# Chunk decays of a two-direction state-space scan: the two directions' exponents merged by a predicated copy before one exponential, and the diagonal weights made in the in-projection

## The reference

```python
a_cs = jnp.cumsum(a, axis=-1)            # a = dt * A, per chunk of 128 positions
Lmat = segsum_exp(a)                     # exp(a_cs[l] - a_cs[s]) for s <= l, else 0
y_diag = jnp.einsum('bclgn,bcsgn,bgrcls,bcsgrp->bclgrp', Cc, Bc, Lmat, xd)
...
y_f = ssd_scan(xs, dt_f, A[0], Bm, Cm)
y_b = flip(ssd_scan(flip(xs), flip(dt_b), A[1], flip(Bm), flip(Cm)))
y = y_f + y_b + xs * d_skip[:, None]
```

## Time and profile before

| | |
|---|---|
| median of 3 runs | 2932.55 us (2932.18 to 2933.72) |
| profiled execution, span | 2927.1 us |
| PE busy in it | 2844.0 us, 97% |
| DVE busy | 1921.0 us, 66% |
| ACT busy | 1161.9 us, 40% |
| POOL busy | 442.2 us, 15% |
| mean granted TensorE clock | 0.984 of full |
| 16 heads, first exponent product to last evacuation | 454.63 to 531.64 us |

### The profile page before, as it was taken

One profiled execution on the slowest core, in us unless ns is written; L12 is line 12 of the kernel. 1 busy time (PEld: TensorE's weight loads), 2 busy tenths in 40 slices (PEclk: granted clock), 3 DMA queues, 4 the chain that ended last, 5 costly groups with the idle time before them and its releaser, 6 DMA issues.

```text
span 2927.1 us, 34428 instructions
## 1 busy us (share of the span) xinstructions
PE 2844.0 (97%) x13489; PEld 2265.7 (77%) x13489; DVE 1921.0 (66%) x2492; ACT 1161.9 (40%) x1708; POOL 442.2 (15%) x323
## 2 busy tenths in 40 slices
PE   8999999999999999999999999999799999999999
PEld 6767778767778888877767888888676888887887
DVE  6548866656587666765667766776737866666254
ACT  2223325213343333433245565556624433334342
POOL 0420011360004332202000000000000232222020
PEclk7999999999999999999999999999999999999999
DMA  6344475025132222375540111111133222226453
GB/s 216 110 136 151 145 224 194 29 79 201 54 131 80 75 86 87 124 251 183 176 157 18 47 43 43 43 43 45 64 101 101 87 86 87 87 65 203 136 158 116
DMA packets 361686, 326.60 MB, mean 112 GB/s; under 512 B 11501, under 2 KB 319182, under 8 KB 361486
## 3 DMA queue, kind: packets, MB, share of 16 engines
q1 hardware_dynamic: 348486, 271.61, 29.7%
q0 software_dynamic: 12000, 48.61, 4.5%
q10 hardware_dynamic: 1040, 4.19, 0.4%
HBM read 263.88 MB, written 68.35 MB: 114 GB/s over the span
## 4 chain that ended last, share of the span: by engine, by line
PE 90%; DVE 5%; ACT 2%; DMA 1%; issue 1%; POOL 1%; SPq 0%; ACTq 0%; DVEq 0%; POOLq 0%
PE psum_gemm L1953 20%; PE psum_misc L1953 18%; PE psum_gemm L2399 8%; PE psum_gemm L216 6%; PE psum_gemm L217 6%; PE psum_gemm L220 6%; PE psum_misc L2463 3%; PE psum_gemm L2484 3%; PE psum_gemm L2472 3%; PE psum_gemm L318 2%; PE psum_misc L216 2%; PE psum_misc L217 2%; PE psum_misc L220 2%; PE psum_misc L888 1%; PE psum_gemm L2485 1%
## 5 line engine op out<-in xcount | busy, mean ns | idle before, releaser
L216 PE MATMUL psum_gemm<-h_hi,w_hi 128*128 128x512 f32 x816 | 329.3, 404 | 12.0 <-DVE h_lo L401 8.2
L217 PE MATMUL psum_gemm<-h_lo,w_hi 128*128 128x512 f32 x816 | 318.5, 390 | 0.0
L198 ACT ACTIVATE w_hi<-w_raw 128x1024 fp32r<-128x1024 f32 x93 | 97.8, 1055 | 455.1 <-PE psum_gemm L220 321.4
L1878 DVE TENSOR_TENSOR ring_lo<-piece_raw,ring_hi 128x512 fp32r<-128x512 f32 x192 | 137.0, 722 | 206.2 <-ACT ring_hi L1872 205.7
L220 PE MATMUL psum_gemm<-h_hi,w_lo 128*128 128x512 f32 x816 | 251.9, 390 | 0.0
L203 DVE TENSOR_TENSOR w_lo<-w_raw,w_hi 128x1024 fp32r<-128x1024 f32 x93 | 119.1, 1285 | 158.5 <-ACT w_hi L198 158.5
L1872 ACT ACTIVATE ring_hi<-piece_raw 128x512 fp32r<-128x512 f32 x192 | 112.7, 593 | 246.2 <-PE psum_misc L1953 208.3
L1953 PE MATMUL psum_misc<-h_hi,ring_hi 128*128 128x512 f32 x512 | 200.6, 392 | 0.6 <-DVE ring_lo L1878 0.6
L216 PEld LDWEIGHTS psum_gemm<-h_hi,w_hi 128*128 128x128 f32 x816 | 153.2, 188 | 61.5 <-issue 20.8
L1953 PE MATMUL psum_misc<-h_hi,ring_lo 128*128 128x512 f32 x512 | 199.4, 389 | 0.0
L1953 PE MATMUL psum_misc<-h_lo,ring_hi 128*128 128x512 f32 x512 | 199.2, 389 | 0.0
(11 more groups left out here) (422 smaller groups left out, 6792.3 us busy)
## 6 DMA issues: line engine op xcount, KB each, us to landing
ada_w<-in_w_ada SPq DMA_DIRECT2D x28, 1024.0 KB, 5.5
w_raw<-in_f_w_up SPq DMA_DIRECT2D x52, 512.0 KB, 4.9
ffn_act_scratch<-gate_act SPq DMA_DIRECT2D x42, 512.0 KB, 2.6
piece_raw<-in_f_w_down SPq DMA_DIRECT2D x80, 256.0 KB, 3.2
piece_raw<-ffn_act_scratch SPq DMA_DIRECT2D x80, 256.0 KB, 2.9
pair_raw<-in_f_w_up SPq DMA_DIRECT2D x36, 512.0 KB, 5.1
w_raw<-in_e_w_in SPq DMA_DIRECT2D x29, 512.0 KB, 4.5
x_scratch<-x_res SPq DMA_DIRECT2D x3, 4096.0 KB, 12.6
```

The costliest lines, as they stand in the source:

```text
L198: act.activation(w_hi[:, s], w_raw[:, s], ACT.Copy).then_inc(s_hi, 1)
L216: pe.matmul(o, wh, rh[:, k, c], start=(k == 0), stop=False)
L217: pe.matmul(o, wh, rl[:, k, c], start=False, stop=False)
L1878: dve.tensor_tensor(Al[:, idx % 7, 0:n], src, Ah[:, idx % 7, 0:n].bitcast(F32), ALU.subtract).then_inc(s_wl, 1)
```

## The change

For each head only the exponents without a mask are made: 4 products for each direction instead of 6 (`exponent`). The forward plane is `pG[:, 1]` for even heads and `pM[:, 0]` for odd ones, the backward plane is always `pG[:, 0]`. DVE copies the backward plane over the forward one where a 128x128 predicate (`above`, 1 above the diagonal) says so, PSUM to PSUM, for all 8 chunks in one instruction. ACT takes one exponential of the merged plane, and DVE multiplies it by the scores one head later (`weights`). The addition of the two directions is gone. `y_of` has two half planes (`pM[:, 1]`) instead of four; scores and B transposes all use `pM[:, 1]`.

The backward direction's term on the diagonal is now missing from the weights. It is score(l,l) * dt_b, a factor of x, like the skip term; both are put into `yS` ahead: `own_scores` (POOL, two multiplications of 128x1024, elementwise C*B), `own_pe` (PE, 16 products of 128x128 by 1 column which sum them over the state, in the hook of `cumsum_pe`), `own_dve` (DVE, four small instructions, giving `y_w` = dt_b * score + d_skip) and `own_x` (POOL, `yS` = `xS` * `y_w`, one 128x1024 multiplication for each of 8 chunks: chunks 0, 1, 4, 5 behind the store of z tile 6, chunks 2, 3, 6, 7 at the end of `diag_pool`). `evac` adds the head's product to `yS`, and waits for all of these. The six coefficients and the shift splits of `mods_dve` go into `coefs_dve`, at head 8. Of the constants, one select and two copies of POOL are gone.

```diff
                 if j == 5:
+                    own_dve(dve)
                     cumsum_dve(dve)
...
                     ssd_consts(pool)
+                    own_scores(pool)
+                if j == 6:
+                    for c in (0, 1, 4, 5):
+                        own_x(pool, c)
...
-        mask = at("mask", AR + 65, [P, 2, P])
-        maskR = at("mask_r", AR + 66, [P, 2, P], F32R)
-        identR = at("ident_r", AR + 67, [P, P], F32R)
+        above = at("above_diagonal", AR + 66, [P, P])
...
+        y_w = at("own_weight", AR + 75.25, [P, CH, 16])
+        g_own = at("own_score", AR + 75.75, [P, SSM_GROUPS, CH])
+        own = at("own_product", AR + 16, [P, SSM_GROUPS, SEQ])
...
-        E_ = at("decays", 32, [P, 2, 2, SEQ])
+        E_ = at("decays", 32, [P, 2, SEQ])
...
+            pool.affine_select(out=above[:], in_=above[:], compare_op=ALU.is_ge, fill=1.0, base=0,
+                               pattern=[[1, P]], channel_multiplier=-1).then_inc(s_sc, 1)
...
-            pool.tensor_copy(maskR[:], mask[:]).then_inc(s_sc, 1)
-            pool.tensor_copy(identR[:], ident[:]).then_inc(s_sc, 1)
             pool.tensor_copy(selR[:], sel[:]).then_inc(s_sc, 1)
-            pool.wait_ge(s_sc, n + 3)
-            pool.tensor_copy(T2[64:128, :], mask[64:128, 0, P - 1:P].to_broadcast([64, SEQ])).then_inc(s_sc, 1)
-            assert n + 4 == NC_CONST
+            pool.wait_ge(s_sc, n + 1)
+            pool.tensor_copy(T2[64:128, :], above[64:128, P - 1:P].to_broadcast([64, SEQ])).then_inc(s_sc, 1)
...
             pe.wait_ge(s_sc, NC_CONST)
+            own_pe(pe)
             for d in range(2):
                 pe.matmul(pM[:, 0, d * P:(d + 1) * P], tri[:, d], aS[:, :, d * 16:(d + 1) * 16], start=True, stop=True)
             pe.matmul(pM[:, 0, 512:768], ones[:], aS[:], start=True, stop=True).then_inc(s_cs2, 1)
...
         def scores_pe(pe, g):
             for c in range(CH):
                 cc = slice(c * P, (c + 1) * P)
-                last = pe.matmul(pM[:, 1 - g, cc], xbc[:, 8 + g, cc], xbc[:, 10 + g, cc], start=True, stop=True)
+                last = pe.matmul(pM[:, 1, cc], xbc[:, 8 + g, cc], xbc[:, 10 + g, cc], start=True, stop=True)
             last.then_inc(s_bt, 1)
...
         def b_turn(pe, h):
...
-                    last = pe.transpose(pM[:, 1 - h, o:o + P], xbc[:, 8 + g, c * P:(c + 1) * P], ident[:])
+                    last = pe.transpose(pM[:, 1, o:o + P], xbc[:, 8 + g, c * P:(c + 1) * P], ident[:])
...
         def scores_act(act, g):
-            act.wait_ge(s_bt, g + 2)
-            act.activation(Gm[:, g], pM[:, 1 - g], ACT.Copy).then_inc(s_gm, 1)
+            act.wait_ge(s_bt, 2 * g + 2)
+            act.activation(Gm[:, g], pM[:, 1], ACT.Copy).then_inc(s_gm, 1)
...
         def b_copy(dve, h):
-            dve.wait_ge(s_bt, h + 4)
-            dve.tensor_copy(BS[:, 4 * h:4 * h + 4].rearrange("p c n -> p (c n)"), pM[:, 1 - h]).then_inc(s_bc, 1)
-
-        def diff(d):
-            return pG[:, 1 - d]
+            dve.wait_ge(s_bt, 2 * h + 3)
+            dve.tensor_copy(BS[:, 4 * h:4 * h + 4].rearrange("p c n -> p (c n)"), pM[:, 1]).then_inc(s_bc, 1)
+
+        def forward(h):
+            return (pG[:, 1], pM[:, 0])[h % 2]
+
+        backward = pG[:, 0]
+
+        def y_ps(h):
+            return pM[:, 1, (h % 2) * HALF:(h % 2) * HALF + HALF]
 
         def diag_pe(pe):
             def y_of(h):
-                if h >= 4:
-                    pe.wait_ge(s_yev, h - 3)
+                if h >= 2:
+                    pe.wait_ge(s_yev, h - 1)
                 elif h == 0:
-                    pe.wait_ge(s_bc, 2)
-                elif h == 2:
                     pe.wait_ge(s_mods, 4)
                 pe.wait_ge(s_M, h + 1)
-                ps = pM[:, (h % 4) // 2, (h % 2) * HALF:(h % 2) * HALF + HALF]
+                ps = y_ps(h)
                 for c in range(CH):
                     last = pe.matmul(ps[:, c * 64:(c + 1) * 64], W_[:, h % 4, c * P:(c + 1) * P],
                                      xS[:, c, h * 64:(h + 1) * 64], start=True, stop=True)
                 last.then_inc(s_y, 1)
+
+            def exponent(h, d):
+                hd = 16 * d + h
+                dst = backward if d else forward(h)
+                for n in range(2):
+                    pe.matmul(dst[:, n * HALF:(n + 1) * HALF], selR[:, hd:hd + 1].to_broadcast([P, P]),
+                              T2[:, n * HALF:(n + 1) * HALF], start=True, stop=False)
+                for n in range(2):
+                    pick = pickR[:].rearrange("p (c h) -> p c h", h=8)[:, 4 * n:4 * n + 4, h % 8:h % 8 + 1]
+                    last = pe.matmul(dst[:, n * HALF:(n + 1) * HALF], csbT[:, 2 * d + h // 8],
+                                     pick.to_broadcast([P, 4, P]), start=False, stop=True)
+                last.then_inc(s_dif[d], 1)
...
             for h in range(SSM_HEADS):
-                for d in range(2):
-                    hd = 16 * d + h
-                    if h >= 1:
-                        pe.wait_ge(s_exp, 2 * h - 1 + d)
-                    elif d:
-                        ev_in_wait(pe, U_OUTB + 1)
-                    for n in range(2):
-                        pe.matmul(diff(d)[:, n * HALF:(n + 1) * HALF], selR[:, hd:hd + 1].to_broadcast([P, P]),
-                                  T2[:, n * HALF:(n + 1) * HALF], start=True, stop=False)
-                    for n in range(2):
-                        pick = pickR[:].rearrange("p (c h) -> p c h", h=8)[:, 4 * n:4 * n + 4, h % 8:h % 8 + 1]
-                        pe.matmul(diff(d)[:, n * HALF:(n + 1) * HALF], csbT[:, 2 * d + h // 8],
-                                  pick.to_broadcast([P, 4, P]), start=False, stop=False)
-                    for n in range(2):
-                        last = pe.matmul(diff(d)[:, n * HALF:(n + 1) * HALF], identR[:],
-                                         maskR[:, d:d + 1].to_broadcast([P, 4, P]), start=False, stop=True)
-                    last.then_inc(s_dif[d], 1)
-                if h == 0:
+                if h >= 2:
+                    pe.wait_ge(s_exp, h - 1)
+                exponent(h, 0)
+                if h:
+                    pe.wait_ge(s_sum, h)
+                else:
+                    ev_in_wait(pe, U_OUTB + 1)
+                exponent(h, 1)
+                if h in (0, 2):
+                    b_turn(pe, h // 2)
+                elif h == 1:
+                    pe.wait_ge(s_bc, 1)
                     scores_pe(pe, 1)
-                elif h < 3:
-                    b_turn(pe, h - 1)
                 elif h == 3:
-                    pe.wait_ge(s_bc, 1)
+                    pe.wait_ge(s_bc, 2)
                     mods_pe(pe)
-                if h >= 3:
+                elif h == 4:
+                    y_of(0)
+                if h >= 4:
                     y_of(h - 3)
             y_of(SSM_HEADS - 3)
             y_of(SSM_HEADS - 2)
@@ -1475,14 +1490,14 @@
         def diag_act(act):
             act.wait_ge(s_red, ADA_END)
             act.activation(dec[:], totS[:], ACT.Exp).then_inc(s_ex, 1)
+            scores_act(act, 0)
             for h in range(SSM_HEADS):
-                for d in range(2):
-                    if h >= 2:
-                        act.wait_ge((s_sum, s_M)[d], h - 1)
-                    act.wait_ge(s_dif[d], h + 1)
-                    act.activation(E_[:, h % 2, d], diff(d), ACT.Exp).then_inc(s_exp, 1)
-                if h < 2:
-                    scores_act(act, h)
+                if h >= 2:
+                    act.wait_ge(s_M, h - 1)
+                act.wait_ge(s_sum, h + 1)
+                act.activation(E_[:, h % 2], forward(h), ACT.Exp).then_inc(s_exp, 1)
+                if h == 1:
+                    scores_act(act, 1)
 
         def diag_pool(pool):
             pool.wait_ge(s_used, U_OUTB)
@@ -1490,32 +1505,79 @@
             pool.wait_ge(s_fs, 16)
             skew = bass.AP(tensor=f_dram.tensor, offset=P - 1, ap=[[2048, ATT_HEADS], [-1, P], [1, STRIP]])
             pool.dma_start(skew_dram, skew).then_inc(s_fs, 16)
+            pool.wait_ge(s_ex, 3)
+            pool.wait_ge(s_csc, 10)
+            for x in range(2):
+                pool.wait_ge(s_zs[x], 64)
+            for c in (2, 3, 6, 7):
+                own_x(pool, c)
+
+        def own_scores(pool):
+            pool.wait_ge(s_sc, NC_CONST)
+            for x in range(2):
+                pool.wait_ge(s_xsc[x], 4)
+            for g in range(SSM_GROUPS):
+                pool.tensor_tensor(own[:, g], xbc[:, 8 + g], xbc[:, 10 + g], ALU.mult).then_inc(s_own, 1)
+
+        def own_x(pool, c):
+
+            pool.wait_ge(s_ownw, 4)
+            pool.tensor_tensor(as_heads(yS[:, c]), as_heads(xS[:, c]),
+                               y_w[:, c].rearrange("p (h o) -> p h o", o=1).to_broadcast([P, 16, 64]), ALU.mult
+                               ).then_inc(s_own, 1)
+
+        def own_pe(pe):
+            pe.wait_ge(s_own, SSM_GROUPS)
+            for g in range(SSM_GROUPS):
```

(57 more changed lines are left out.)

17 lines of the change are left out of this document (8 added, 9 removed).

## The result

The changed kernel takes 2954.99 us (median of 4 runs, 2944.92 to 2958.6) against 2932.36 before: a ratio of 1.0074, 95% interval [1.0063, 1.0086]. It is slower by about 22 us, where 2932.0 us was forecast and the range ended at 2940.5. The profiled execution has a span of 2956.9 us (2927.1 before) and a mean granted clock of 0.975 (0.984).

A forecast was written before the change was run, and what follows sets the result against it. PE's own work was taken to bound the diagonal stage. A stage gain of 7.2 us against an in-projection loss of 6.7 gave a span of 2926.6 and, with the median 5.4 above it, 2932.0 us; range 2926.0 to 2940.5.

The forecast's parts named there:

- PE's work and the heads: Diagonal stage: dropping two mask pairs a head saves 14.8 us of PE over 16 heads; period 3.57 us, PE-bound.
- The slower rival, two passes of the plane: DVE's merge needs two PSUM passes, distance 2.2 us, 4.0 us a head; 8.5 us more, 2940.5 us; chance 0.16.
- The first heads: Heads 0 to 5 of the diagonal stage: 18.2 us of PE work plus waits of 1.1, 2.5 and 2.0 us.
- weights 1 and weights 2 each meet a running `own_x` and lose about 1.5 us: First heads: DVE's weights of heads 1 and 2 take 2.7 us instead of 1.2 beside POOL's multiplications.
- forecast waits of 2.5 and 2.0 us: First heads: PE's second wait (B copy, head 3) and third (first output, for `mods_dve`); 1.0 and 0.4 without POOL.
- The last batch: In-projection's end: four `own_x` delay DVE's last batch by 6.4 us, so PE waits 3.3 us at L518.
- `own_pe`: 3.4 us forecast: In-projection: 16 one-column products, 32 trace instructions, cost PE 2 x 1.71 = 3.4 us, all on the path.
- The weight side sets the pace: `own_pe` in the in-projection: one-column products cost as much as output products, 8 about 1.71 us; one column saves nothing.
- The tail: From the last backward products to the last evacuation: 9.5 us, 1.55 longer than before, the price of two half planes.
- The coefficients at head 8: Diagonal stage: about 0.85 us of small DVE instructions exceed PE's margin of 0.24 us, costing 0.6 us.
- The forecast's -0.5: Whole span: in-projection loses 6.7 us (3.4 `own_pe`, 3.3 wait at L518), diagonal stage gains 7.2; span 2926.6.
- 7.2 + 3.0 + 1.55: Diagonal stage: forecast gain 7.2 us, POOL collisions in the first heads 3.0, two half planes' price in the tail 1.55.

The follow-up runs named there:

- e1_turns: Changed kernel with waits ahead of POOL's diagonal-stage multiplications, so that one set of DVE's weights lies between two of them: 2943.7 us, ratio 1.0047.
- e10_best: Changed kernel with POOL waits, first `own_x` held until the bias chain is done, `own_pe` spread out later, own places for last three outputs: 2932.5 us, ratio 1.0005.
- e14_one_wait: Changed kernel with one wait, for DVE's weights 0, directly ahead of the diagonal stage's first `own_x`: 2947.8 us, ratio 1.0055.
- e18_behind_dma: Changed kernel with one wait for weights 0, placed ahead of POOL's DMA issue L1507, then `own_x`: 2955.7 us (one run; before 2927.8).
- e11_spread_late: Changed kernel with `own_pe`'s products spread two by two between projection k-steps, late enough that POOL's own scores are done: 2953.4 us, ratio 1.0073.
- e9_tail: Changed kernel with places of their own for the last three outputs, 13 to 15: 2946.0 us, ratio 1.0057.
- e16_order: e10_best with the stage's first `own_x` ahead of POOL's DMA issues and the second `x_w` one head later: 2926.1 us, ratio 0.9985.

## Why the prediction was wrong

**PE's work and the heads: right.** The mask pairs are gone and the period is 3.57 us. One head of the kernel after, answering to the earlier trace rows, and DVE in it, to the earlier trace rows:

```profile
530.22 1.89 PE L1445 MATMUL psum_misc<-x_S,chunk_weights 128*128 128x64 f32 x16
...
533.80 1.89 PE L1445 MATMUL psum_misc<-x_S,chunk_weights 128*128 128x64 f32 x16
...
530.49 1.23 DVE L1571 COPY_PREDICATED psum_gemm<-above_diagonal,psum_gemm 128x1024 f32<-128x1024 uint32 x1 [0.61 <-PE psum_gemm L1457]
531.63 1.22 DVE L1563 TENSOR_TENSOR chunk_weights<-decays,G_scores 128x1024 f32<-128x1024 f32 x1
532.76 0.68 DVE L1555 TENSOR_TENSOR y_S<-y_S,psum_misc 128x512 f32<-128x512 f32 x1
```

533.80 - 530.22 = 3.58. The merge lasts 1.23 us, its distance is 1.14, as taken. The slower rival, two passes of the plane, did not occur; the slower outcome came by another way, which was given no case. The Trainium skill, page VectorE: DVE Perf Modes, section Why PSUM operands drop a tier, speaks of one read port into PSUM; these rows show no second pass of a predicated copy over it.

**The first heads: wrong, and the largest miss, 13.2 us.** The failed step is "weights 1 and weights 2 each meet a running `own_x` and lose about 1.5 us". It took the price of one collision from the earlier trace rows and laid it where the layout saw an overlap. It was weights 0, which the layout had free, and DVE got no turn at all over six multiplications: 11.2 us of POOL's time in one piece. In place of the forecast waits of 2.5 and 2.0 us PE waited 10.1 and 0.2: 5.8 more. The remaining 7.4 is half clock, which set in during that wait and which PE pays from 488.7 to about 504 (0.53 from 490 to 505); the working had no term for it. Where the row is broken up the step takes 490.49 - 466.27 = 24.2 us in e1_turns and 482.38 - 458.32 = 24.1 in e10_best, forecast 24.0. That is in part luck: the waits are shorter than forecast (0.8 and 1.9 us in e1_turns, where the forecast had 2.5 and 2.0), and 1.7 us of half clock fill the gap. The Trainium skill, page SBUF — State Buffer, section Who interferes with whom, says that GpSimd and VectorE share an exclusive port pair, that the one to issue first holds it for the whole instruction, and that a VectorE instruction with at most one SBUF input does not contend outside the two-port modes. In e14_one_wait a merge (data in PSUM, predicate in SBUF) takes 1.23 us at 475.83, beside `own_x`, and the weights behind it 2.77, which agrees. What the starving rows show is more than it says, and e18_behind_dma measures it: no turn between two multiplications. Nor do they show the first to issue served: the record of weights 0 starts at 474.51, 0.69 us ahead of the first `own_x` but beside a DMA issue of POOL (474.07 to 475.18), and ends behind all six; whether that issue held the ports is open.

**The last batch: right in place, 2.7 us short.** PE waited at L517 for the batch, as said, 4.4 us instead of 3.3, since DVE lost all 7.49 us of the four `own_x` and not 4 x 1.57; here too a DMA issue (448.02, 0.53 us) stands directly ahead of the row. The other 1.6 us are half clock behind the wait.

**`own_pe`: 3.4 us forecast, 6.8 measured.** "The weight side sets the pace" held: 3.49 us in the row of e1_turns, at full clock, 3.7 spread out. What was missing is that the clock fell late in a row of one-column products and stayed at 0.50 behind it, here until 442.6: 0.43 us for each product instead of 0.23.

**The tail: 9.5 us forecast, 13.9 measured.** The waits were foreseen (output 13 starts 3.28 us behind T, forecast 3.33), the half clock behind them (0.50 from 546 on) was not: the whole 4.4. The coefficients at head 8 cost 0.6, as forecast (two periods of 4.09 and 3.69 us there instead of 3.57).

**What the misses share.** 7.4, 1.6 and 4.4 us from waits of PE on, and 3.3 (6.8 less the 3.49 that the row takes at full clock) from the one-column row on: about 17 of the 23.7 us are half clock, and the working priced a wait at its length. How long the half clock lasts also differs between the runs, and it is likely to be part of their spread: the same wait of 10.1 us ended at 486.75, 487.52 and 488.67 in e11_spread_late, e9_tail and the changed kernel, and the clock was back some 6, 15 and 15 us later. One stretch of each (the clock is the third number), first e11_spread_late, then the changed kernel:

```profile
492.00:494.00 2.00, 2.00 (x15) 0.86 0.54 219
```

```profile
500.00:502.00 2.00, 2.00 (x10) 0.50 0.51 215
```

So the stage is 81.2 us in one and 87.4 in the other, with the same code in it. Not every wait brings it: those of e16_order, up to 1.41 us, left the clock at 1.00, where 1.38 us in the changed kernel's tail did not.

**The sum.** The forecast's -0.5 was a gain of 7.2 against a loss of 6.7. e10_best gains 5.3 us in the stage and loses 3.7 ahead of it, which looks near but is another sum: with the collisions and the tail's waits away the forecast's own terms give 7.2 + 3.0 + 1.55 = 11.8 us in the stage. Waits of 0.7, 1.9 and 2.1 us and two stretches of half clock stand between. e16_order, which has neither stretch, gains 11.1 and loses 4.1 ahead: there the forecast's terms hold within 1 us.

## What to carry to other kernels

Price a float32 multiplication of 128x1024 on GpSimd beside VectorE's instructions with two SBUF inputs at its full duration (1.9 us here), and a row of them behind a DMA issue as one block; put a wait for VectorE between them, or begin them where VectorE works from PSUM. Price a wait of TensorE, or a row of one-column products on it, with the half clock that may come with it, which here cost between nothing and 7.4 us. When small work is taken off the busiest engine, lay out on the clock which queue it lands in and what stands next to it there.

## What the hardware did that was not expected

- Beside four multiplications of GpSimd behind a DMA issue (with two more behind them) VectorE's instruction took 11.36 us; beside the same six behind a wait it took 2.77 us, 1.22 alone. In the code only the order of one wait and one DMA issue differs; with it the instruction comes 0.9 or 2.1 us behind the first multiplication.
- The clock of TensorE fell to half late in or just behind a row of 32 products of 128x128 by one column, with no wait in it (0.87 from 435 to 436 and 0.50 from 436 to 442, the row ending at 437.00), and did not where they stood four by four between products of 512 columns (1.00 from 410 to 450 in e11_spread_late).
- A predicated copy from PSUM to PSUM of 128x1024 float32, with a mask that repeats every 128 elements, takes 1.23 us, as long as a plain copy out of PSUM (1.22).
